# The mLSTM's queries and keys in 12 blocks of 128 features shared by heads, the decays' products one to a step

## The chip, the cores and the metric

The kernel runs on one core of one Trainium2 chip. The metric is the device time of a whole execution in microseconds: 1609.09 us, the median of three runs (1609.03 to 1609.48). What follows is about a stretch of some 125 us in the middle of it.

## What is computed

Two transformer blocks run over one sequence of 256 positions with 1024 features. The first has two layers; its second layer mixes positions with an mLSTM of 4 heads of 192 features, and this is the part that changes. Cut to that part:

```
u = x @ w_in_mlstm                      # 256 x 3336: q 768, k 768, v 768, o 768, gates 8, memory query 256
qk = silu(causal_dwconv(qk, qk_conv_w)) # 4 taps over positions, one weight per feature and tap
q, k = split(qk)                        # 4 heads of 192 features each
log_d = bcum[t] - bcum[s] + log_i[s]    # decay of position s seen from t, causal, stabilised
sc = (q_h . k_h * 192**-0.5) * exp(log_d - m)
h  = (sc @ v_h) / max(|sum(sc)|, exp(-m))
h  = layer_norm(h, per head) * head_norm_g
tok = sigmoid(o_pre) * h
x  = layer_norm(alpha * x + [tok, memory attention] @ w_out)
```

Silu and the taps work feature by feature, so it does not matter to them which features share a tile. Only `q_h . k_h` needs the 192 features of one head.

## The kernel before

Every weight matrix is cut by hand into a list of tiles (`weight_tiles`), of at most 128 x 2048 values, and the four engines walk this one list. SP fetches a tile into one of 4 `raw` buffers. ScalarE (ACT) rounds it to `whi`, VectorE (DVE) forms the rest `wlo`, and each has 3 buffers, so a tile can be prepared when TensorE (PE) is done with the tile three before it. Preparation runs two tiles ahead (`LOOK`). Each product is then made of three matmuls (high x high, high x low, low x high). Each engine's program is written out in order, and waits are on counters (`need.wait_ge`); what stands behind a waiting instruction on the same engine waits too.

PE's results go to 8 PSUM banks. The first four (`psw`) are handed out in turn by `bank(...)`: who claims one waits until the result that was in it four claims before has been taken out. The last four (`psy`) hold the wide results (`big_rows`).

Around the change the order is this. Gates and memory query; four tiles of values (`big_rows("v")`); the queries and keys; four tiles of output gates (`big_rows("o")`); then four tiles of the output projection (`big_rows("out1")`), the second of which waits for the finished heads. For queries and keys, head h and part 0 (q) or 1 (k) is one weight tile of 192 columns, so 8 tiles. `pair` on PE (L782 to L788) makes from it two blocks of 96 features x 256 positions in one bank: 2 blocks x 8 row blocks x 3 products = 48 matmuls of 256 columns. `head` on ACT (L1293) copies both blocks to `zp` and writes the last tap into `qk`; `head` on DVE (L1891) adds the other three taps with six instructions; `head_silu` (L1307) applies Silu in place. `qk[h % 2]` has two buffers. Between two tiles each engine does one entry of its list `steps`:

- `turn`, `value`, `finish`: the memory attention of the same layer, one head to a step.
- `weights(h)`: PE spreads the decay row of head h over the partitions (L751), ACT makes Exp of it twice (L1285), into `wt`; POOL then clears what is not causal (L2392). Before, all four heads are in the first step.
- `attend(h)`: PE multiplies keys and queries of head h (L757), DVE scales the product with `wt` into `sc` (L1904).
- `states(h)`: PE multiplies `sc` and values (L768), DVE forms the denominators and the statistics, ACT the divided copy `hb` between them (L1912, L1312), POOL normalises `hb` by the statistics, head after head and behind all four `weights` (the loop at L2403).

After the last `states`, ACT makes the sigmoid of the output gates (L1338), DVE multiplies it with the normalised heads in four pieces (L1942, L1944), PE turns the product (`mlstm_turned`, `headT`), ACT and DVE split it into high and low (`mhi`, `mlo`), and the second tile of `out1` can start. ACT functions come from tables: where Exp and Silu follow each other, an ACT_TABLE_LOAD stands between; copies need none.

Of the kernel before, what the change touches and what calls it, by code (L numbers as in the profile page):

```python
# [11 lines left out]
T = 256  # L12
# [15 lines left out]
def weight_tiles():  # L28
    tiles = []
# [93 lines left out]
PARAMS = [("conv_w", 18), ("qkconv", 64), ("conv_dw", 124), ("conv_b", 4), ("conv_g", 4), ("conv_lb", 4),  # L123
# [132 lines left out]
def program(nc, A, out):  # L256
# [5 lines left out]
    with ctx:  # L262
# [124 lines left out]
        zp = [arena.take(2 * 259).rearrange("p (b n) -> p b n", b=2)[0:96] for _ in range(2)]  # L387
        qk = [[arena.take(2 * T).rearrange("p (b n) -> p b n", b=2)[0:96] for _ in range(2)], [hf[0:96, s, :, :] for s in range(2)]]
# [110 lines left out]
        def tensor(e):  # L499
# [235 lines left out]
            def mlstm_mixer():  # L735
# [21 lines left out]
                def attend(h):  # L757
                    q_, k_ = qk[h % 2]
                    b = bank("attend", h)
                    for part in range(2):  # L760
                        need.wait_ge(*act.at("qk", h, part))
                    for f in range(2):
                        mm(b[:, 0:256], k_[:, f, 0:128], q_[:, f, :], f == 0, f == 1)
                    for f in range(2):
                        ins = mm(b[:, 256:384], k_[:, f, 128:256], q_[:, f, 128:256], f == 0, f == 1)
                    ins.then_inc(*pe.up(("bank", ("attend", h))))

                def states(h):  # L768
# [371 lines left out]
        def scalar(e):  # L1140
# [132 lines left out]
            def mlstm_mixer():  # L1273
# [19 lines left out]
                def head(h, part):  # L1293
                    b = place["head", h, part]
                    q_ = qk[h % 2][part]
                    need.wait_ge(*pe.at("bank", ("head", h, part)))
                    if h:
                        need.wait_ge(*dve.at("taps", h - 1, part))
                    copy(zp[part][:, :, 3:259], blocks(b[0:96, :], 256)).then_inc(*act.up(("zp", h, part)))
                    if h > 1:  # L1300
                        need.wait_ge(*pe.at("bank", ("attend", h - 2)))
                    for f in range(2):
                        blk = 8 * part + 2 * h + f
                        ins = copy(q_[:, f, :], b[0:96, 256 * f:256 * f + 256], scale=qwt[0:96, blk, 3:4])
                        ins.then_inc(*act.up(("tap3", h, part, f), *([took(("head", h, part))] if f else [])))

                def head_silu(h, part):  # L1307
                    q_ = qk[h % 2][part]
                    need.wait_ge(*dve.at("taps", h, part))
                    e.activation(q_, q_, ACT.Silu).then_inc(*act.up(("qk", h, part)))  # L1310
# [14 lines left out]
                steps = [lambda: (turn(1, 0), [weights(h) for h in range(4)]), lambda: turn(1, 1), lambda: turn(1, 2),  # L1325
# [1346 lines left out]
```

## Time and profile before

| | |
|---|---|
| median of three runs | 1609.09 us |
| the profiled execution, its own time | 1608.99 us |
| its span in the profile | 1607.2 us |
| PE, DVE, ACT, POOL busy, share of the span | 96%, 71%, 56%, 6% |
| mean granted clock of TensorE | 0.986 |
| the mLSTM's queries and keys | 721.5 to 784.2 us of the span |

The span is what the profile covers; the 1.8 us between it and the execution's own time lie around it. Times in the rows below are from the span's start. In a timeline a row merges instructions of one kind that follow each other: start, duration, engine, line, operation, what is written and read, how many, and in brackets how long the engine stood idle before it and on whom. Matmuls are pipelined: one of 256 columns is shown as 0.28 us long, but the next starts 0.12 us after it, so the spacing of starts is what a matmul costs.

### The profile page before, as it was taken

The page shows a single profiled execution, that of the slowest core. Times are in us where ns is not written, and L with a number is a line of the kernel's source. Part 1 is how long each engine was busy: PE and PEld are TensorE (multiplying, and loading weights), DVE is VectorE, ACT ScalarE, POOL GpSimd, SP SyncE. Part 2 cuts the span into 40 slices and gives each one's busy share as a digit, 9 for nine tenths or more (in the row PEclk, how much of TensorE's full clock was granted, in tenths as well). Part 3 has the DMA queues.
Part 4 walks back from the last instruction along what each step waited for, and adds up shares of the span by engine and source line. Part 5 has one row for each costly group of instructions (what it writes and reads, how often), then busy time and mean ns, then how long its engine had stood idle before and what let it go on. Part 6 is the DMA issues. An engine that isn't in the chain of part 4 may idle for free.

```text
span 1607.2 us, 22098 instructions
## 1 busy us (share of the span) xinstructions
PE 1543.8 (96%) x8926; PEld 1358.6 (85%) x8926; DVE 1138.4 (71%) x1628; ACT 897.7 (56%) x1356; POOL 101.8 (6%) x137
## 2 busy tenths in 40 slices
PE   7999999999999999999999999798999989999996
PEld 6888899888888888889978888797999778888885
DVE  5666666666667666655776566769867878989997
ACT  5455454455545555456545555444456657777774
POOL 0000000000000000001300000042002320000000
PEclk9999999999999999999999999899999999999998
DMA  9655454555555555343455554335334659999992
GB/s 359 211 191 197 159 196 162 195 218 197 186 183 198 196 183 191 138 148 101 160 207 222 189 197 162 133 125 210 131 106 164 234 210 350 354 347 345 359 368 103
DMA packets 48059, 332.99 MB, mean 207 GB/s; under 512 B 5712, under 2 KB 5840, under 8 KB 10192
## 3 DMA queue, kind: packets, MB, share of 16 engines
q1 hardware_dynamic: 46496, 321.43, 55.0%
q0 software_dynamic: 1456, 10.09, 1.6%
q8 instruction: 72, 1.18, 0.3%
q14 instruction: 35, 0.29, 0.1%
HBM read 330.45 MB, written 1.05 MB: 206 GB/s over the span
## 4 chain that ended last, share of the span: by engine, by line
PE 83%; DVE 10%; ACT 3%; POOL 1%; issue 1%; DMA 0%; SPq 0%; DVEq 0%; ACTq 0%; POOLq 0%
PE psw L505 54%; PE psy L505 28%; DVE wlo L1650 4%; DVE kT L2037 2%; PE psw L508 1%; ACT whi L1147 1%; POOL ar L2434 1%; DVE xs L1659 0%; DMA raw<-in_ws 0%; ACT xs L1147 0%; ACT ar L1147 0%; DVE x L1733 0%; POOL rstd L2354 0%; DVE gsel L2227 0%; DVE x L1746 0%
## 5 line engine op out<-in xcount | busy, mean ns | idle before, releaser
L1650 DVE TENSOR_TENSOR wlo<-raw,whi 128x1024 fp32r<-128x1024 f32 (+2 forms) x552 | 640.5, 1206 | 192.2 <-ACT whi L1147 186.7
L505 PE MATMUL psw<-xs,whi 128*128 128x512 f32 (+3 forms) x2544 | 687.3, 345 | 18.5 <-DVE wlo L1650 8.5
L1147 ACT ACTIVATE whi<-raw 128x1024 fp32r<-128x1024 f32 (+2 forms) x552 | 540.0, 1031 | 150.2 <-PE psy L505 107.0
L505 PE MATMUL psw<-xs,wlo 128*128 128x256 f32 (+2 forms) x1928 | 516.3, 282 | 2.1 <-DVE xs L1659 2.1
L505 PEld LDWEIGHTS psw<-xs,whi 128*128 128x128 f32 (+2 forms) x2544 | 427.4, 187 | 68.8 <-DVE wlo L1650 8.5
L505 PEld LDWEIGHTS psw<-xs,wlo 128*128 128x128 f32 (+2 forms) x1928 | 362.9, 188 | 17.4 <-issue 2.6
L505 PE MATMUL psw<-whi,xs 128*128 128x512 f32 (+1 forms) x704 | 178.9, 365 | 6.3 <-DVE xs L1659 5.1
L505 PE MATMUL psy<-whi,hhi 128*128 128x512 f32 x472 | 158.0, 390 | 0.0
L505 PE MATMUL psy<-whi,hlo 128*128 128x512 f32 x472 | 157.8, 389 | 0.0
L505 PE MATMUL psy<-wlo,hhi 128*128 128x512 f32 x472 | 157.7, 389 | 0.0
L505 PEld LDWEIGHTS psw<-whi,xs 128*128 128x128 f32 x704 | 126.0, 190 | 27.6 <-issue 2.6
L1147 ACT ACTIVATE ar<-psw 128x256 f32<-128x256 f32 (+3 forms) x127 | 56.3, 445 | 144.7 <-PE psw L505 131.4
L505 PE MATMUL psw<-wlo,xs 128*128 128x512 f32 (+1 forms) x352 | 106.6, 362 | 0.0
L505 PEld LDWEIGHTS psy<-whi,hlo 128*128 128x128 f32 x472 | 88.6, 188 | 18.5
L505 PEld LDWEIGHTS psy<-wlo,hhi 128*128 128x128 f32 x472 | 88.6, 188 | 18.4
L505 PEld LDWEIGHTS psy<-whi,hhi 128*128 128x128 f32 x472 | 88.6, 188 | 17.4
L1147 ACT ACTIVATE hf<-psw 128x256 f32<-128x256 f32 x82 | 31.0, 384 | 116.7 <-PE psw L505 116.7
L1688 DVE TENSOR_TENSOR hf<-hf,psw 128x256 f32<-128x256 f32 x82 | 34.0, 418 | 77.6 <-ACT hf L1147 77.6
L2354 POOL TENSOR_TENSOR rstd<-ve,mhalf 128x1 f32<-128x1 f32 x18 | 12.6, 699 | 1163.6 <-DVE ve L1739 1163.6
L1650 DVE TENSOR_TENSOR wlo<-ar,whi 128x1024 fp32r<-128x1024 f32 x64 | 74.4, 1222 | 4.9 <-ACT whi L1147 4.9
L505 PEld LDWEIGHTS psw<-wlo,xs 128*128 128x128 f32 x352 | 66.7, 190 | 10.4
L1693 DVE TENSOR_TENSOR ar<-ar,psw 128x256 f32<-128x256 f32 x82 | 34.3, 418 | 54.5 <-ACT ar L1147 54.5
(303 smaller groups left out, 1624.2 us busy)
## 6 DMA issues: line engine op xcount, KB each, us to landing
raw<-in_ws SPq DMA_DIRECT2D x252, 1024.0 KB, 4.8
ar<-in_ws SPq DMA_DIRECT2D x32, 1024.0 KB, 6.5
raw<-in_ws SPq DMA_DIRECT2D x17, 768.0 KB, 4.3
gb<-in_ln POOLq DMA_DIRECT2D x8, 1024.0 KB, 6.1
raw<-in_ws SPq DMA_DIRECT2D x4, 672.0 KB, 3.9
ar<-in_memT SPq DMA_DIRECT2D x2, 1024.0 KB, 13.7
ar<-in_xT SPq DMA_DIRECT2D x2, 512.0 KB, 5.4
raw<-in_ws SPq DMA_DIRECT2D x2, 512.0 KB, 6.3
```

The source lines that it names most:

```text
L505: return e.matmul(o, l, rr, start=start, stop=stop)
L508: return e.transpose(o, i, ident[0:n, 0:n])
L1147: return e.activation(o, i, ACT.Copy, **k)
L1650: e.tensor_tensor(wlo[i % NS][:, c0:c1], raw_t[slot[i]][:, c0:c1], whi[i % NS][:, c0:c1].bitcast(f32), ALU.subtract).then_inc(*made.up((i, ...
L1688: e.tensor_tensor(hf[:, s, j, :], hf[:, s, j, :], place["fgate", f, c, j][:, 0:256], ALU.add).then_inc(*dve.up(("fgate", f, c, j), took((" ...
L1693: then(e.tensor_tensor(corr[j], corr[j], place["up", f, c, j][:, 0:256], ALU.add), took(("up", f, c, j)))
L2037: ins = e.scalar_tensor_tensor(out=ca[:, b, :], in0=zc[:, b, tap:tap + 256], scalar=dwt[:, b, tap:tap + 1], in1=ca[:, b, :], op0=ALU.mult, ...
L2354: e.tensor_tensor(rstd[:, t:t + 1], ve[:, t:t + 1], mhalf[:, 0:1], ALU.pow).then_inc(*pool.up(("rstd", n, t)))
L2434: then(e.tensor_tensor(dst[:, lo:272], src[:, lo:272], src[:, lo - step:272 - step], ALU.add))
```

## The change

Queries and keys are made in tiles of 256 columns, j = 0 to 2, each for q and k: 6 tiles of two blocks of 128 features. A head's 192 features are then one whole block and half of another: head 0 has block 0 and the first half of block 1, head 1 the second half of block 1 and block 2, and so on. `attend(h)` still makes two products per result, over 128 and over 64 features instead of twice 96. The tap weights are laid out by 128 (`qkconv` shrinks from 64 to 48 columns). There are six steps instead of eight: `weights(h)` goes one head to a step (steps 0, 1, 3, 4), `attend(2)`, `attend(3)` stand together behind the first tile of output gates and `states(2)`, `states(3)` together behind the second. As `qk` has two buffers, tile pair 2 overwrites pair 0, and ACT's write of its last tap waits for `attend(1)`.

```diff
-    for h in range(4):
+    for j in range(3):
         for part in range(2):
-            n = 768 * part + 192 * h
-            tiles.append(("w_in_mlstm", (0,), 0, 8, n, n + 192))
+            n = 768 * part + 256 * j
+            tiles.append(("w_in_mlstm", (0,), 0, 8, n, n + 256))
...
                 def attend(h):
-                    q_, k_ = qk[h % 2]
+                    rows = [(192 * h, 192 * h + 128), (192 * h + 128, 192 * h + 192)] if h % 2 == 0 else [
+                        (192 * h, 192 * h + 64), (192 * h + 64, 192 * h + 192)]
                     b = bank("attend", h)
                     for part in range(2):
-                        need.wait_ge(*act.at("qk", h, part))
-                    for f in range(2):
-                        mm(b[:, 0:256], k_[:, f, 0:128], q_[:, f, :], f == 0, f == 1)
...
+                        need.wait_ge(*act.at("qk", (192 * h + 191) // 256, part))
+                    at = [(qk[r0 // 256 % 2], r0 // 128 % 2, r0 % 128, (r1 - 1) % 128 + 1) for r0, r1 in rows]
+                    for f, ((q_, k_), blk, p0, p1) in enumerate(at):
+                        mm(b[:, 0:256], k_[p0:p1, blk, 0:128], q_[p0:p1, blk, :], f == 0, f == 1)
...
-                steps = [lambda: (turn(1, 0), [weights(h) for h in range(4)]), lambda: (value(1, 0), turn(1, 1)),
-                         lambda: (attend(0), value(1, 1), turn(1, 2)), lambda: (states(0), value(1, 2), turn(1, 3)),
-                         lambda: (attend(1), value(1, 3)), lambda: (states(1), finish(1)), lambda: attend(2), lambda: states(2)]
-                for h in range(4):
+                steps = [lambda: (turn(1, 0), weights(0)), lambda: (value(1, 0), turn(1, 1), weights(1)),
+                         lambda: (attend(0), value(1, 1), turn(1, 2)), lambda: (states(0), value(1, 2), turn(1, 3), weights(2)),
+                         lambda: (attend(1), value(1, 3), weights(3)), lambda: (states(1), finish(1))]
+                for j in range(3):
                     for part in range(2):
-                        pair(("head", h, part), Tile("w_in_mlstm", 768 * part + 192 * h), xhi, xlo, x_rows(4), m=96)
+                        pair(("head", j, part), Tile("w_in_mlstm", 768 * part + 256 * j), xhi, xlo, x_rows(4))
                         steps.pop(0)()
                 big_rows("o", "w_in_mlstm", 4, xhi, xlo, lambda j, k: x_rows(4)(k), splits, 2304,
-                         {0: lambda: attend(3), 1: lambda: states(3)})
+                         {0: lambda: (attend(2), attend(3)), 1: lambda: (states(2), states(3))})
...
-                    copy(zp[part][:, :, 3:259], blocks(b[0:96, :], 256)).then_inc(*act.up(("zp", h, part)))
-                    if h > 1:
-                        need.wait_ge(*pe.at("bank", ("attend", h - 2)))
...
+                    copy(zp[part][:, :, 3:259], blocks(b[:, :], 256)).then_inc(*act.up(("zp", j, part)))
+                    if j > 1:
+                        need.wait_ge(*pe.at("bank", ("attend", 1)))
...
-                steps = [lambda: (turn(1, 0), [weights(h) for h in range(4)]), lambda: turn(1, 1), lambda: turn(1, 2),
-                         lambda: (states(0), turn(1, 3)), lambda: None, lambda: (states(1), finish(1)), lambda: None, lambda: states(2)]
...
+                steps = [lambda: (turn(1, 0), weights(0)), lambda: (turn(1, 1), weights(1)), lambda: turn(1, 2),
+                         lambda: (states(0), turn(1, 3), weights(2)), lambda: weights(3), lambda: (states(1), finish(1))]
...
-                w.rows(4, {0: lambda: attend(3), 1: lambda: states(3)})
+                w.rows(4, {0: lambda: (attend(2), attend(3)), 1: lambda: (states(2), states(3))})
```

(The first two lists of steps are PE's and ACT's; DVE's loses its last two entries, `attend(2)` and `states(2)`, in the same way.)

On ACT, the first two tiles of queries and keys. L1289 and L1290 are the Exps of one head's decays, L1310 the Silu. Before:

```order
L1147 ACTIVATE ar<-psw 96x2x256 [waits s_pe]
L1147 ACTIVATE ar<-psw,par 96x256 x2
L1147 ACTIVATE ar<-psw 128x512 [waits s_pe]
L1289 ACTIVATE ar<-psw,ar 128x256 [waits s_pe]
L1290 ACTIVATE ar<-psw,ar 128x128
...
L1289 ACTIVATE ar<-psw,ar 128x256 [waits s_pe]
L1290 ACTIVATE ar<-psw,ar 128x128
L1310 ACT_TABLE_LOAD
L1310 ACTIVATE ar<-ar 96x512 [waits s_dve]
```

Now (the same lines are L1291, L1292 and L1313, and the copies are L1149):

```order
L1149 ACTIVATE ar<-psw 128x2x256 [waits s_pe]
L1149 ACTIVATE ar<-psw,par 128x256 x2
L1149 ACTIVATE ar<-psw 128x512 [waits s_pe]
L1291 ACTIVATE ar<-psw,ar 128x256 [waits s_pe]
L1292 ACTIVATE ar<-psw,ar 128x128
L1313 ACT_TABLE_LOAD
L1313 ACTIVATE ar<-ar 128x512 [waits s_dve]
...
L1149 ACTIVATE ar<-psw,par 128x256 x2
L1149 ACTIVATE ar<-psw 128x512 [waits s_pe]
L1291 ACT_TABLE_LOAD
L1291 ACTIVATE ar<-psw,ar 128x256 [waits s_pe]
L1292 ACTIVATE ar<-psw,ar 128x128
L1313 ACT_TABLE_LOAD
L1313 ACTIVATE ar<-ar 128x512 [waits s_dve]
```

The three later heads' Exps have moved behind later tiles, and each is now enclosed by two table loads; six loads are added in all.

On PE, the work between the first two tiles; the product that spreads a head's decay row is `psw<-ar 128x256`. Before:

```order
L508 MATMUL psw<-par,gb 128x128 [waits s_dve]
L508 MATMUL psw<-par,gb 128x128 x3
L505 MATMUL psw<-ar 128x256 [waits s_pool,s_act]
L505 MATMUL psw<-ar 128x256 [waits s_act] x3
L505 MATMUL psw<-xs,whi 96x256 [waits s_wlo,s_act]
```

Now:

```order
L508 MATMUL psw<-par,gb 128x128 [waits s_dve]
L508 MATMUL psw<-par,gb 128x128 x3
L505 MATMUL psw<-ar 128x256 [waits s_pool,s_act]
L505 MATMUL psw<-xs,whi 128x256 [waits s_wlo,s_act]
...
L505 MATMUL psy<-vm,ar 128x64 [waits s_act]
L505 MATMUL psy<-vm,ar 128x64 x3
L508 MATMUL psw<-par,gb 128x128 x4
L505 MATMUL psw<-ar 128x256
L505 MATMUL psw<-xs,whi 128x256 [waits s_wlo,s_act]
```

The products of all four heads stood here, three of them behind waits for ACT; now one stands here, without the waits, and the other three have gone behind later tiles.

## Rows read from the trace of the kernel before

**Rows 1.** Busy time by engine, part 1 of the page.

```profile
PE 1543.8 (96%) x8926; PEld 1358.6 (85%) x8926; DVE 1138.4 (71%) x1628; ACT 897.7 (56%) x1356; POOL 101.8 (6%) x137
```

**Rows 2.** Timeline of PE, 128-feature tile of the memory query, and what follows.

```profile
695.09 0.40 PE L505 MATMUL psw<-xs,whi 128*128 128x256 f32 x2
...
700.85 0.52 PE L505 MATMUL psy<-whi,xs 128*128 128x384 f32 x2
```

**Rows 3.** Timeline of PE, queries and keys, first steps.

```profile
721.54 0.48 PE L505 MATMUL psw<-xs,whi 128*96 128x256 f32 x2
...
727.83 1.12 PE L505 MATMUL psw<-ar 4*128 4x256 f32 x4
...
729.95 1.36 PE L505 MATMUL psw<-ar 4*128 4x256 f32 x4 [1.00 <-ACT ar L1147]
...
731.25 0.74 PE L505 MATMUL psw<-xs,whi 128*96 128x256 f32 x2
...
738.32 1.00 PE L505 MATMUL psy<-vm,ar 128*128 128x64 f32 x8
...
739.53 0.48 PE L505 MATMUL psw<-xs,whi 128*96 128x256 f32 x2
...
745.26 1.47 PE L505 MATMUL psw<-ar 96*128 96x256 f32 x8
```

**Rows 4.** Stretches: from:to, length, busy of PE, PEld, DVE, ACT, POOL, PEclk, DMA.

```profile
731.00:732.00 1.00, 1.00 (x4) 0.76 (x4) 1.00 (x4) 1.00 (x4) 0.93 (x3) 0.50 0.52 197
...
804.00:808.00 4.00, 2.92 (x13) 2.44 (x14) 3.86 (x9) 2.72 (x4) 0.73 (x2) 1.00 1.01 360
```

**Rows 5.** Timeline of ACT, queries and keys.

```profile
728.57 0.61 ACT L1147 ACTIVATE ar<-psw 96x512 f32<-96x512 f32 x1
...
729.76 0.62 ACT L1147 ACTIVATE ar<-psw 128x512 f32<-128x512 f32 x1
...
732.05 0.54 ACT L1289 ACTIVATE ar<-psw,ar 128x256 f32<-128x256 f32 x1
...
732.86 1.28 ACT L1310 ACT_TABLE_LOAD   x1
...
734.16 0.63 ACT L1310 ACTIVATE ar<-ar 96x512 f32<-96x512 f32 x1
...
742.08 0.63 ACT L1310 ACTIVATE ar<-ar 96x512 f32<-96x512 f32 x1 [1.67 <-DVE ar L1900]
...
757.66 0.73 ACT L1147 ACTIVATE r<-psw,ar 128x192 f32<-128x192 f32 x2 [2.63 <-DVE ar L1917]
...
796.83 2.00 ACT L1147 ACTIVATE whi<-raw 128x1024 fp32r<-128x1024 f32 x2
```

**Rows 6.** Timeline of DVE, taps of one tile.

```profile
754.70 2.46 DVE L1900 SCALAR_TENSOR_TENSOR hf<-ar,par,hf 96x256 f32<-96x256 f32 x6 [2.53 <-ACT hf L1147]
```

**Rows 7.** Timeline of POOL, heads 2 and 3.

```profile
789.98 4.33 POOL L2405 TENSOR_SCALAR r<-r,ar 128x192 f32<-128x192 f32 x2
...
797.90 0.71 POOL L2403 TENSOR_TENSOR ar<-ar,mhalf 128x2 f32<-128x2 f32 x1 [3.60 <-DVE ar L1925]
...
798.72 5.39 POOL L2405 TENSOR_SCALAR r<-r,ar 128x192 f32<-128x192 f32 x2
```

**Rows 8.** Timeline of DVE, after the last head.

```profile
807.49 0.56 DVE L1944 TENSOR_TENSOR r<-r,ar 128x384 f32<-128x384 f32 x1
...
807.97 2.35 DVE L1650 TENSOR_TENSOR wlo<-raw,whi 128x1024 fp32r<-128x1024 f32 x2
...
811.91 1.89 DVE L1659 TENSOR_TENSOR mlo<-psw,mhi 128x512 fp32r<-128x512 f32 x3 [1.59 <-ACT mhi L1147]
```

**Rows 9.** Timeline of PE, states of head 3 and output projection.

```profile
794.44 1.14 PE L505 MATMUL psw<-ar 128*128 128x193 f32 x6
...
795.28 0.65 PE L505 MATMUL psy<-whi,xs 128*128 128x384 f32 x2
...
812.75 0.70 PE L505 MATMUL psy<-whi,mhi 128*128 128x512 f32 x2 [0.63 <-DVE mlo L1659]
```

More of the change, by code:

```diff
@@ L386, in program @@
         qwt = P("qkconv").rearrange("p (b w) -> p b w", w=4)
-        zp = [arena.take(2 * 259).rearrange("p (b n) -> p b n", b=2)[0:96] for _ in range(2)]
-        qk = [[arena.take(2 * T).rearrange("p (b n) -> p b n", b=2)[0:96] for _ in range(2)], [hf[0:96, s, :, :] for s in range(2)]]
+        zp = [arena.take(2 * 259).rearrange("p (b n) -> p b n", b=2) for _ in range(2)]
+        qk = [[arena.take(2 * T).rearrange("p (b n) -> p b n", b=2) for _ in range(2)], [hf[:, s, :, :] for s in range(2)]]
         sc = [arena.take(384) for _ in range(2)]
@@ L1291, in weights, with head, head_silu @@
                                  scale=-1.0).then_inc(*act.up(("decay", h), took(("decay", h))))
[L1293 to L1298, printed above, removed]
-                    copy(zp[part][:, :, 3:259], blocks(b[0:96, :], 256)).then_inc(*act.up(("zp", h, part)))
-                    if h > 1:
-                        need.wait_ge(*pe.at("bank", ("attend", h - 2)))
-                    for f in range(2):
[L1303 to L1310, printed above, removed]
+                def head(j, part):
+                    b = place["head", j, part]
+                    q_ = qk[j % 2][part]
+                    need.wait_ge(*pe.at("bank", ("head", j, part)))
+                    if j:
+                        need.wait_ge(*dve.at("taps", j - 1, part))
+                    copy(zp[part][:, :, 3:259], blocks(b[:, :], 256)).then_inc(*act.up(("zp", j, part)))
+                    if j > 1:
+                        need.wait_ge(*pe.at("bank", ("attend", 1)))
+                    for f in range(2):
+                        blk = 6 * part + 2 * j + f
+                        ins = copy(q_[:, f, :], b[:, 256 * f:256 * f + 256], scale=qwt[:, blk, 3:4])
+                        ins.then_inc(*act.up(("tap3", j, part, f), *([took(("head", j, part))] if f else [])))
+                def head_silu(j, part):
+                    q_ = qk[j % 2][part]
+                    need.wait_ge(*dve.at("taps", j, part))
+                    e.activation(q_, q_, ACT.Silu).then_inc(*act.up(("qk", j, part)))
                 def states(h):
@@ L1324, in mlstm_mixer @@
                              blocks(place["y", "v", 2 * t + i][:, 0:384], 192)).then_inc(*act.up(took(("y", "v", 2 * t + i)), ("va",)))
-                steps = [lambda: (turn(1, 0), [weights(h) for h in range(4)]), lambda: turn(1, 1), lambda: turn(1, 2),
-                         lambda: (states(0), turn(1, 3)), lambda: None, lambda: (states(1), finish(1)), lambda: None, lambda: states(2)]
-                for h in range(4):
+                steps = [lambda: (turn(1, 0), weights(0)), lambda: (turn(1, 1), weights(1)), lambda: turn(1, 2),
+                         lambda: (states(0), turn(1, 3), weights(2)), lambda: weights(3), lambda: (states(1), finish(1))]
+                for j in range(3):
                     for part in range(2):
                         w.tile()
-                        head(h, part)
+                        head(j, part)
                         steps.pop(0)()
-                        head_silu(h, part)
-                w.rows(4, {1: lambda: states(3)})
+                        head_silu(j, part)
+                w.rows(4, {1: lambda: (states(2), states(3))})
                 for t in range(2):
@@ L1889, in decay_columns, with head @@
                     e.tensor_copy(ac, blocks(place["decays",][:, 0:16], 8)).then_inc(*dve.up(took(("decays",))))
-                def head(h, part):
-                    q_ = qk[h % 2][part]
+                def head(j, part):
+                    q_ = qk[j % 2][part]
                     need.wait_ge(*pool.at("zp", part))
@@ L1895, in head @@
                         for f in range(2):
[L1896 to L1897 removed]
+                            blk = 6 * part + 2 * j + f
+                            need.wait_ge(*act.at("tap3", j, part, f))
                             if s:
[L1899 to L1900 removed]
+                                need.wait_ge(*dve.at("tap", j, part, s - 1, f))
+                            e.scalar_tensor_tensor(out=q_[:, f, :], in0=zp[part][:, f, s:s + 256], scalar=qwt[:, blk, s:s + 1],
                                                    in1=q_[:, f, :], op0=ALU.mult,
[L1902 removed]
+                                                   op1=ALU.add).then_inc(*dve.up(("tap", j, part, s, f), ("taps", j, part)))
                 def attend(h):
@@ L1929, in mlstm_mixer @@
                 steps = [lambda: None, lambda: None, lambda: attend(0), lambda: states(0), lambda: (attend(1), scale(1)),
-                         lambda: (states(1), finish(1)), lambda: attend(2), lambda: states(2)]
-                for h in range(4):
+                         lambda: (states(1), finish(1))]
+                for j in range(3):
                     for part in range(2):
                         w.tile()
-                        head(h, part)
+                        head(j, part)
                         steps.pop(0)()
-                w.rows(4, {0: lambda: attend(3), 1: lambda: states(3)})
+                w.rows(4, {0: lambda: (attend(2), attend(3)), 1: lambda: (states(2), states(3))})
                 need.wait_ge(*hn_in.at("hn"))
```

13 lines of the change are left out of this document (4 added, 9 removed).

## The prediction

> **What bounds the kernel now.** I read the busy times first: TensorE (PE) works 96% of the span [rows 1], so time is won where PE has less to do or stops waiting. Then the PE timeline of the queries and keys, the only place the change touches. PE reaches them at 721.54. Up to the weights' products it runs without a gap; then come four such products (two at 727.83, two at 729.95, with 1.00 us of idle time between them that ended with ACT), and the second tile starts at 731.25 [rows 3]. Last, the other engines of the stretch: ACT works there in a long chain per tile (copy, last tap, copy of the memory probabilities, Silu) [rows 5], and DVE's three taps take 2.46 us [rows 6]. They follow PE, and PE asks for their results one step later. So the stage is PE's, but ACT is close behind.
>
> **Term 1, the matmuls: -11.3 us.** A 128-feature tile of 48 matmuls runs from 695.09 to 700.85, 5.76 us [rows 2]. A 96-feature one runs from 739.53 to 745.26, 5.73 us [rows 3]. Fewer output features make a matmul no cheaper, 0.12 us either way. Eight tiles at 5.73 are 45.8, six at 5.76 are 34.6. The difference is 11.3 us of PE, all on the path.
>
> **Term 2, the burst of decay products: -2.6 us.** Two heads' products, issued without waiting, take about 1.05 us, since four instructions of rows 3 run 0.26 us apart; so four heads would be done at 729.93, and the next tile starts at 731.25: 1.3 us of waits. That tile then takes 7.07 us, 731.25 to 738.32, instead of 5.73: 1.34 us more [rows 3]. The granted clock shows why: 0.50, the 1.2 GHz level, from 731 to 732 [rows 4]. Before it fell, PE had idled and worked on products with 4 rows. Now one product stands there, and its bank has been emptied before. Both parts go.
>
> **Term 3, ACT's longer chain: +2.4 us.** The decays' Exps now come one head to a step, each between a load of the Exp table and one of the Silu table: six loads more, at 1.28 us each [rows 5], 7.7 us of ACT. ACT and DVE also prepare tiles a third larger: two halves of 1024 take ACT 2.00 us [rows 5], so three quarters of it, 1.5, before. Three larger tiles are prepared before ACT gets to the first queries, 1.5 us of ACT together, and DVE's part of them also delays the score maxima for which ACT waits, by about as much as one tile's growth, 0.5. So I put ACT's first copy at 730.6 instead of 728.57 [rows 5]. From there the steps are laid end to end.
> - One head's Exps: 0.80 us, 732.05 to the load at 732.86 [rows 5]. First tile: copies 1.3, memory copy 0.6, Exps 0.8, load 1.3, Silu 0.6: done at 735.0. Second tile: preparation 1.95 (736.9), copies (738.2), memory copy (738.8), load, Exps and load 3.4 (742.2), Silu: 742.8.
> - PE: first tile to 727.3, transposes and one product 1.05, tile to 734.1, the value and transposes 1.2 (738.32 to 739.53) [rows 3] and a product 0.5, tile to 741.6. `attend(0)` needs the Silu of 742.8: PE waits 1.2 us. Before, that Silu began at 742.08 and PE came at 745.26 [rows 3, 5].
> - The same again at `attend(1)`. PE leaves the fourth tile at 751.2, does the states of head 0, value, transposes and a product (2.7), and the fifth tile ends at 759.7. ACT from 751.2: copies to 752.6, DVE's taps 2.46 [rows 6] to 755.0, denominators and divided copies 1.2 as from the end of the taps at 757.16 to 758.39 [rows 5, 6], memory copy, load, Exps, load, Silu: 760.9. PE waits 1.2 us.
>
> Bounds: nothing if ACT has caught up by then; at most 2.6 each, if both switches of a step fall wholly on PE. I take 1.2 twice, as the steps give it. Behind `attend(2)` there is none: one tile of output gates stands between it and the last queries, and the last step has no Exps.
>
> **Here the Trainium skill speaks against the change.** The row shows the load starting 0.01 us after the last Exp's end and Silu 0.02 us after the load's [rows 5]: 1.28 us in all. The page "ScalarE: Activation LUTs" (What ACT_TABLE_LOAD costs) gives about 1.28 us for the load and 1.38 for a drain, 2.66 for every switch, and advises doing all of one set before switching. By it ACT would get 16.0 us more instead of 7.7, and the sum would be about 1604.8.
>
> **Term 4, the end of the heads: +2.0 us.** Now `states(2)` and `states(3)` come together, so POOL gets its last two heads together. Output gate tile 3 starts at 795.28, 0.84 us after `states(3)` [rows 9], and POOL starts head 3 at 797.90 and is done at 804.11 [rows 7]. By terms 1 to 3 PE is about 11.5 us earlier at 795.28, at 783.8. Head 2's states are ready 0.84 us earlier than head 3's, and DVE needs about 2.2 for one head, so POOL starts head 2 at 785.3. It takes 0.8 and 4.33, until 790.5; head 3 another 0.8 and 5.39, until 796.7 [rows 7]. That is 7.4 us earlier than before, while PE is 11.5 earlier. DVE's last product ends at 808.05, then it prepares a tile (2.35), then writes the rest for which PE waits until 812.75 [rows 8, 9]. From 796.7 this gives 800.7, 803.0, and with the first rest 803.8 for PE, against 801.2 if nothing were late: 2.6. With POOL at 4.33 also for head 3 it is 1.5. I take 2.0; the bounds are 0.5 and 3.5, since POOL's pace changes with what DVE does.
>
> **At no cost.** The attend products over 128 and 64 instead of 96 and 96 rows: as many instructions, columns unchanged, under 1.5 us per head [rows 3]; a gain or loss of some 0.1. DMA: the same bytes in fewer transfers, issued four tiles ahead, six tiles of 5.8 us. ACT's last tap of pair 2 waits for `attend(1)`; PE is done with it while ACT still prepares a tile. Copies, taps and Silus, 8 sets before and 6 now, save work beside PE.
>
> **The sum.** -11.3 - 2.6 + 2.4 + 2.0 = -9.5 us. The profiled execution took 1608.99 for a span of 1607.2, 0.1 below the median; so 1599.5 for it and **1599.6** for the median. What follows in the kernel moves forward unchanged.
>
> **Rivals.**
> 1. *ACT has caught up* and term 3 is nothing: 1597.2. For it: idle time on ACT in these steps, 1.67 us before the Silu at 742.08 [rows 5]. Against: it is used in the sum already. Chance 0.08.
> 2. *The clock falls once or twice at the new waits.* A wait of 1.2 us, then attend products, narrow values and transposes, looks a little like what came before 731. Against it, 1.1 us of idle time in 804 to 808 left the clock at 1.00 [rows 4]. Price 1.3 us each as in term 2: 1600.9 or 1602.2. Chance 0.20.
> 3. *A switch of tables costs twice its row*, the page's rule: two switches stand before each of the two Silus for which PE waits, so 2 x 2.6 more: 1604.8. For it no row; the load of rows 5 shows 1.28. Chance 0.06, and with a fall of the clock on top it passes 1605.9.
> 4. *Slower: the low clock stays.* After the wait at `attend(0)`, with waits, small products and waits following, the clock stays at 1.2 GHz for the three remaining tiles and on. At half the clock a tile takes up to twice its 5.76 us. Break-even is at 1.7 tiles; with three, 17.2 us: 1616.8. Against: the fall at 731 was over within one tile, which cost only 1.34 [rows 3]. Chance 0.02.
>
> That the change doesn't do what it says (a 128-wide tile costs more, or the wider last block adds passes) is excluded by rows 2.
>
> **How the numbers follow.** Forecast 0.64, rivals 0.08, 0.20, 0.06, 0.02. The range runs from rival 1 to just over two falls of the clock, with term 4's bounds in it: 1597.0 to 1602.8; left out are rivals 3 and 4 and the coincidence of ends, some 0.15. A measurement of this kernel can tell about 0.2%, 3.2 us, from no change. Forecast, rivals 1 and 2 and a third of rival 3 are faster by more: 0.94. The rest of rival 3, with a fall of the clock: 0.04 within. Slower 0.02.
>
> **What would show it.** PE busy down by about 11 us; no idle time and clock 1.00 between the first two tiles; waits of about 1.2 us on ACT's Silu (L1313) ahead of `attend(0)` and `attend(1)`; six more loads of 1.28 us; the second output projection tile waiting 3 to 5 us behind the turned heads, for a chain that begins with POOL's head 3. No wait at the attends, one over 2.5 us, or a PEclk of 0.50 past 740 would make term 3 wrong; POOL done with head 3 more than 8.5 us earlier than before would make term 4 wrong.

## The result, and the profile after

| | before | the change |
|---|---|---|
| median | 1609.28 us (4 runs, 1609.03 to 1610.63) | 1599.66 us (4 runs, 1598.42 to 1601.15) |
| ratio | | 0.9936 (95% interval 0.9924 to 0.9949) |
| the profiled execution: its own time, span | 1608.99, 1607.2 us | 1601.15, 1599.3 us |
| mean granted clock | 0.986 | 0.989 |

The forecast was 1599.6, so the sum was met. Its terms were not: both savings and both costs in it were put too large, a cost that had been put at nothing was 2.45 us, and these misses nearly cancelled. That the two numbers agree to 0.1 us is luck. The page first, the row of busy times:

```profile
PE 1535.0 (96%) x8830; PEld 1345.6 (84%) x8830; DVE 1132.9 (71%) x1612; ACT 902.3 (56%) x1350; POOL 97.3 (6%) x137
```

PE is busy 8.8 us less than in [rows 1]; about 11 had been forecast. Single executions of one kernel lie up to 4.3 us apart (the nine of the kernel before on one chip from 1607.01 to 1611.32), and the profiled one of the change is the slowest of its four. A stage can be compared more sharply than a whole execution, so all that follows is read from one stretch. It begins with the last score products of the memory attention (`psw<-kT`, 720.49 before, 720.34 now), which stand just ahead of the first tile of queries and keys, and ends with the first matmul of the second output projection tile (812.75 in [rows 9], 804.05 now). It took 92.26 us and takes 83.71, 8.55 less. From there to the end of the span it is 194.5 us before (1607.2 - 812.75) and 195.3 now (1599.3 - 804.05), a difference of the size that one kernel shows from run to run.

PE in that stretch, in the timeline:

```profile
721.39 0.51 PE L505 MATMUL psw<-xs,whi 128*128 128x256 f32 x2
...
727.25 0.60 PE L508 MATMUL psw<-par,gb 128*128 128x128 f32 x4
727.78 0.69 PE L505 MATMUL psw<-ar 4*128 4x256 f32 x2
728.41 0.50 PE L505 MATMUL psw<-xs,whi 128*128 128x256 f32 x2
...
734.27 1.00 PE L505 MATMUL psy<-vm,ar 128*128 128x64 f32 x8
...
736.26 0.50 PE L505 MATMUL psw<-xs,whi 128*128 128x256 f32 x2
...
742.77 2.13 PE L505 MATMUL psw<-ar 128*128 128x256 f32 x8 [0.50 <-ACT ar L1313]
744.83 1.10 PE L505 MATMUL psy<-vm,ar 128*128 128x64 f32 x8
...
761.47 0.67 PE L505 MATMUL psw<-ar 64*128 64x256 f32 x2 [0.53 <-ACT hf L1313]
...
763.44 1.00 PE L505 MATMUL psy<-vm,ar 128*128 128x64 f32 x8
...
776.90 0.67 PE L505 MATMUL psw<-hf 128*128 128x256 f32 x2 [0.30 <-ACT ar L1313]
...
786.56 0.66 PE L505 MATMUL psy<-whi,xs 128*128 128x384 f32 x2
...
804.05 0.70 PE L505 MATMUL psy<-whi,mhi 128*128 128x512 f32 x2 [0.63 <-DVE mlo L1662]
```

Start to start, a tile is 5.86 us (721.39 to 727.25, and again 728.41 to 734.27). Between the first two tiles stand only the transposes and one product of 4 rows (727.78, 0.63 us), and nothing is waited for there; in [rows 3] this place had four products and 1.00 us of idle time. At 742.77 and 761.47 the brackets show the new waits for Silu. `attend(0)` takes from 742.77 to 744.83, 2.06 us, where it took 1.31 (745.26 in [rows 3] to 746.57). One line of the kernel before shows that end, the other two the transposes ahead of the burst and ahead of the third tile:

```profile
727.29 0.60 PE L508 MATMUL psw<-par,gb 128*128 128x128 f32 x4
...
739.16 0.61 PE L508 MATMUL psw<-par,gb 128*128 128x128 f32 x4
...
746.57 1.00 PE L505 MATMUL psy<-vm,ar 128*128 128x64 f32 x8
```

The clock was full where it had been 0.50 in [rows 4], and full around the new waits. Stretches of the change, with the columns of [rows 4]:

```profile
728.00:732.00 4.00, 4.00 (x32) 3.67 (x32) 2.42 (x3) 4.00 (x8) 0.00 (x0) 1.00 0.35 141
732.00:736.00 4.00, 4.00 (x35) 3.76 (x33) 2.38 (x6) 3.69 (x7) 0.82 (x2) 1.00 0.55 197
...
740.00:744.00 4.00, 3.50 (x24) 2.66 (x23) 1.16 (x4) 3.97 (x6) 0.54 (x2) 1.00 0.46 181
...
760.00:764.00 4.00, 3.47 (x22) 2.52 (x22) 1.83 (x2) 3.63 (x6) 0.00 (x0) 1.00 0.01 4
```

ACT, from its copy of the first tile on, and at the second one, where the Exps of head 1 stand between two table loads:

```profile
730.35 0.63 ACT L1149 ACTIVATE ar<-psw 128x512 f32<-128x512 f32 x1
...
738.66 1.28 ACT L1291 ACT_TABLE_LOAD   x1
739.95 0.47 ACT L1291 ACTIVATE ar<-psw,ar 128x256 f32<-128x256 f32 x1
740.32 0.36 ACT L1292 ACTIVATE ar<-psw,ar 128x128 f32<-128x128 f32 x1
740.70 1.28 ACT L1313 ACT_TABLE_LOAD   x1
742.00 0.63 ACT L1313 ACTIVATE ar<-ar 128x512 f32<-128x512 f32 x1
```

The end of the heads, POOL and then DVE:

```profile
788.20 0.71 POOL L2406 TENSOR_TENSOR ar<-ar,mhalf 128x2 f32<-128x2 f32 x1 [7.06 <-DVE ar L1918]
789.01 2.01 POOL L2408 TENSOR_SCALAR r<-r,ar 128x192 f32<-128x192 f32 x2
...
792.26 4.45 POOL L2408 TENSOR_SCALAR r<-r,ar 128x192 f32<-128x192 f32 x2
```

```profile
800.47 2.35 DVE L1653 TENSOR_TENSOR wlo<-raw,whi 128x1024 fp32r<-128x1024 f32 x2
```

POOL is done with head 3 at 796.71 (792.26 + 4.45).

### The profile page after: what moved, and what is told of

It reads as the page before. It is cut to its first block, busy times and chain, and to the rows that moved or that the text cites. A ratio compares the mean times of both kernels' runs of the same rounds, so it can differ in the third digit from the quotient of the medians.

```text
span 1599.3 us, 21882 instructions
## 1 busy us (share of the span) xinstructions
PE 1535.0 (96%) x8830; PEld 1345.6 (84%) x8830; DVE 1132.9 (71%) x1612; ACT 902.3 (56%) x1350; POOL 97.3 (6%) x137
## 3 DMA queue, kind: packets, MB, share of 16 engines
HBM read 330.44 MB, written 1.05 MB: 207 GB/s over the span
## 4 chain that ended last, share of the span: by engine, by line
PE 81%; DVE 11%; ACT 4%; POOL 1%; issue 1%; DMA 0%; SPq 0%; DVEq 0%; ACTq 0%; POOLq 0%
PE psw L505 53%; PE psy L505 27%; DVE wlo L1653 4%; DVE kT L2040 2%; PE psw L508 1%; ACT whi L1149 1%; POOL ar L2437 1%; DVE xs L1662 1%; DMA raw<-in_ws 0%; ACT ar L1149 0%; ACT xs L1149 0%; DVE ar L1903 0%; DVE x L1736 0%; POOL rstd L2357 0%; DVE gsel L2230 0%
## 5 line engine op out<-in xcount | busy, mean ns | idle before, releaser
L1653 DVE TENSOR_TENSOR wlo<-raw,whi 128x1024 fp32r<-128x1024 f32 (+3 forms) x548 | 640.0, 1213 | 195.8 <-ACT whi L1149 190.3
L505 PE MATMUL psw<-xs,whi 128*128 128x512 f32 (+2 forms) x2480 | 674.2, 346 | 18.6 <-DVE wlo L1653 8.6
L1149 ACT ACTIVATE whi<-raw 128x1024 fp32r<-128x1024 f32 (+3 forms) x548 | 539.8, 1037 | 148.7 <-PE psy L505 106.7
L505 PE MATMUL psw<-xs,wlo 128*128 128x256 f32 (+1 forms) x1896 | 506.5, 281 | 2.1 <-DVE xs L1662 2.1
L505 PEld LDWEIGHTS psw<-xs,whi 128*128 128x128 f32 (+1 forms) x2480 | 419.6, 189 | 69.7 <-DVE wlo L1653 8.6
L505 PEld LDWEIGHTS psw<-xs,wlo 128*128 128x128 f32 (+1 forms) x1896 | 359.3, 189 | 17.4 <-issue 2.6
L1149 ACT ACTIVATE ar<-psw 128x256 f32<-128x256 f32 (+3 forms) x125 | 55.3, 444 | 136.6 <-PE psw L505 124.0
L1149 ACT ACTIVATE hf<-psw 128x256 f32<-128x256 f32 x82 | 31.2, 386 | 116.4 <-PE psw L505 116.3
```

The source lines that it names most:

```text
L505: return e.matmul(o, l, rr, start=start, stop=stop)
L1149: return e.activation(o, i, ACT.Copy, **k)
L1653: e.tensor_tensor(wlo[i % NS][:, c0:c1], raw_t[slot[i]][:, c0:c1], whi[i % NS][:, c0:c1].bitcast(f32), ALU.subtract).then_inc(*made.up((i, ...
```

## Experiments

Each stretch below is measured as above, in one profiled execution. Times are medians in us, ratios are against runs of the kernel before on the same chip; the kernels ran on several chips. The rows of a product are what it sums over, the first number in `128x256`.

| kernel | stretch | time (runs) | ratio, 95% interval |
|---|---|---|---|
| before | 92.26 | 1609.28 (4) | |
| the change | 83.71 | 1599.66 (4) | 0.9936, 0.9924 to 0.9949 |
| blocks of 128 alone | 86.77 | 1602.49 (4) | 0.9954, 0.9937 to 0.9971 |
| decays one to a step alone | 91.31 | 1607.91 (10) | 0.9989, 0.9979 to 0.9998 |
| no table switches | 82.37 | 1598.40 (2) | 0.9928, 0.9908 to 0.9948 |
| whole blocks in attend | 81.37 | 1596.99 (2) | 0.9919, 0.9899 to 0.9939 |
| 96 and 64 rows in the old layout | 96.87 | 1613.21 (1) | |
| 64 rows only in the old layout | 93.62 | 1609.74 (1) | |
| equal row counts side by side | 82.95 | 1598.51 (5) | 0.9932, 0.9918 to 0.9945 |
| decays early, attend a step later | 82.25 | 1597.95 (5) | 0.9926, 0.9912 to 0.9939 |
| the same, decays in two pairs | 81.14 | 1597.32 (1) | |
| the same, ACT's last step turned round | 79.93 | 1594.95 (5) | 0.9915, 0.9901 to 0.9928 |

The first theory was that the attend products cost more because consecutive products differ in rows, that a table load costs the 1.28 us that its row shows and no more, and that the burst is worth more with the larger blocks than without. The rivals: the 2.45 us come from something else at these places (the clock, a late buffer), and the two halves of the change add up.

### The two halves of the change

Blocks of 128, all decays again in the first step (PE's and ACT's lists):

```diff
-                steps = [lambda: (turn(1, 0), weights(0)), lambda: (value(1, 0), turn(1, 1), weights(1)),
+                steps = [lambda: (turn(1, 0), [weights(h) for h in range(4)]), lambda: (value(1, 0), turn(1, 1)),
```

> The stretch is the time on TensorE from the last score product of the memory attention to the first matmul of the second output projection tile: 92.3 us before, 83.7 with the change. This kernel has the blocks of 128 but all four heads' decay products and Exps in the first step again. Theory: the burst stalls TensorE until ACT has emptied the banks, now later than before, since ACT starts its first copy at 730.4 instead of 728.6, so the second tile starts at about 733 instead of 728.4, at the low clock for some 3 us; against that three products of 0.63 us are no longer between later tiles and the waits for Silu at attend(0) and attend(1), 0.66 and 0.68 us, are gone: stretch 86.5, between 85.5 and 87.5, 2 to 3 us slower than the change. Rival: spreading the decays is worth nothing, because the six table loads it adds cost as much as the burst: within 0.5 us of the change's 83.7.

Blocks of 96 as before, the decays at steps 0, 1, 3 and 4:

```diff
-                steps = [lambda: (turn(1, 0), [weights(h) for h in range(4)]), lambda: (value(1, 0), turn(1, 1)),
+                steps = [lambda: (turn(1, 0), weights(0)), lambda: (value(1, 0), turn(1, 1), weights(1)),
```

> The kernel before, with eight tiles of 96 as it had, and only the decays one head to a step. Theory: the burst and its low clock go (3.42 us between the transposes and the second tile become 0.63, the tile takes 5.73 instead of 7.07), three products of 0.63 us come in later steps, and ACT, which has smaller tiles to prepare and starts 1.8 us earlier than with the change, keeps ahead of TensorE: no wait at the attends, stretch 92.3 - 2.8 - 1.3 + 1.9 + 0.3 = 90.4. Rival: the six table loads alone make the waits at attend(0) and attend(1), whatever the tiles' size: then 91.5 or more.

Measured: 86.77 us (86.5 expected) and 91.31 us (90.4 expected). So the blocks alone give 5.49, the decays alone 0.95, and both together 8.55, 2.1 more than the two added. PE with the blocks alone:

```profile
727.71 1.13 PE L505 MATMUL psw<-ar 4*128 4x256 f32 x4
731.67 2.07 PE L505 MATMUL psw<-ar 4*128 4x256 f32 x4 [2.83 <-ACT ar L1149]
```

Its clock there, in the same columns as above:

```profile
728.00:732.00 4.00, 1.17 (x5) 0.71 (x5) 2.51 (x3) 4.00 (x9) 0.00 (x0) 0.77 0.31 129
732.00:736.00 4.00, 4.00 (x15) 3.16 (x15) 2.31 (x6) 3.97 (x11) 2.65 (x8) 0.50 0.58 197
```

With blocks of 128, ACT is later with its first copies, and the burst waits 2.83 us for it instead of 1.00; then PE runs at 0.50 through the rest of the burst, two products in 2.0 us, and on through the first third of the matmuls of the next tile, which takes 7.31 us (not shown: 733.67 to 740.98) instead of 5.86. With blocks of 96, PE meets ACT a second time, at `attend(1)`:

```profile
741.52 1.47 PE L505 MATMUL psw<-ar 96*128 96x256 f32 x8
...
759.27 1.55 PE L505 MATMUL psw<-hf 96*128 96x256 f32 x8 [0.62 <-ACT hf L1310]
```

There is no wait at `attend(0)`, and the tile before `attend(1)` had its last matmul at 758.37: some 0.8 us are lost on Silu. That is why the decays alone came out 0.9 above what I expected. The rival of that run was half right: the loads make the wait at `attend(1)` with tiles of 96 too, the one at `attend(0)` only with the larger tiles.

### ACT's table loads

The Exps of heads 1 to 3 become copies, so that no function of the Exp table stands there:

```diff
+                    if h:
+                        copy(wt[:, h, 0:256], b[:, 0:256], scale=ac[:, 0, h:h + 1])
+                        copy(wt[:, h, 256:384], b[:, 128:256], scale=ac[:, 1, h:h + 1])
...
+                        return
```

> The change, with the Exps of the decays of heads 1 to 3 replaced by copies scaled by the same column, so that none of the six added table loads is left; the decays of those heads are no decays any more. Theory: ACT is done 2.6 us earlier in each step with decays, the waits at attend(0) and attend(1) vanish (0.66 and 0.68 us), and the stretch is 83.7 - 1.3 = 82.4. Rival: the waits come from the larger tiles (ACT's and DVE's preparation) and stay: 83.7.

```profile
742.35 2.05 PE L505 MATMUL psw<-ar 128*128 128x256 f32 x8
...
760.37 0.70 PE L505 MATMUL psw<-ar 64*128 64x256 f32 x2
```

Both waits are gone and the stretch is 1.34 us shorter. The change's own two waits add up to the same: tile starts at 736.26 and (not shown) 754.94, plus 5.86 each, would have let the attends start at 742.12 and 760.80; they started at 742.77 and 761.47, 0.65 and 0.67 later. So all of what six more loads cost PE is these 1.3 us, of 7.7 that they take on ACT. The third wait for Silu, 0.30 us at `attend(2)` (776.90), is no part of it: it is 0.29 us without the loads, and the kernel before has one of 0.22 at `attend(3)` (not shown: 788.86). The gate tile and the wait behind it take 4.7 us in all three.

### The rows of consecutive products

`attend` with 128 rows in all of its products, in both blocks that hold a part of the head. A head's product then takes in features of its neighbour, so this kernel serves for its time alone:

```diff
-                    at = [(qk[r0 // 256 % 2], r0 // 128 % 2, r0 % 128, (r1 - 1) % 128 + 1) for r0, r1 in rows]
+                    at = [(qk[r0 // 256 % 2], r0 // 128 % 2, 0, 128) for r0, r1 in rows]
```

> The change, with the attend products over all 128 rows of both blocks of a head instead of 128 and 64, so that a head's product takes in 64 features of its neighbour. More rows, same number of instructions and columns. Theory A (what costs is a change in the number of rows between products that follow each other, about 0.2 us each, four to a head): the four attends take 5.1 us together as before, not 7.6, and the stretch is 83.7 - 2.5 = 81.2. Theory B (the blocks of 128 are dearer than those of 96, or products out of two tile pairs are): no change, 83.7, or more.

```profile
742.73 1.55 PE L505 MATMUL psw<-ar 128*128 128x256 f32 x8 [0.49 <-ACT ar L1313]
744.11 1.00 PE L505 MATMUL psy<-vm,ar 128*128 128x64 f32 x8
```

`attend(0)` takes 1.38 us instead of 2.06, at the same place, behind the same wait, with as many products and columns. The stretch is 2.34 shorter. The weight loads show where the time is. The change, then the kernel before:

```profile
742.74 0.30 PEld L505 LDWEIGHTS psw<-ar 128*128 128x128 f32 x2 [0.67 <-ACT ar L1313]
743.37 0.29 PEld L505 LDWEIGHTS psw<-ar 64*128 64x128 f32 x2 [0.33 <-issue]
744.00 0.71 PEld L505 LDWEIGHTS psw<-ar 128*128 128x128 f32 x4 [0.33 <-issue]
```

```profile
745.15 1.40 PEld L505 LDWEIGHTS psw<-ar 96*128 96x128 f32 x8
```

With 96 rows in each, the eight loads run on without a gap. In the change there is an idle time of 0.33 us, ended by no other engine, before the load of 64 rows and again before the one of 128; with whole blocks the eight loads take 1.38 us without one (not shown).

Then the same question with neither the blocks nor the moved decays: in the kernel before, the second block of each head with 64 rows instead of 96, and, in a second kernel, both with 64.

```diff
-                    for f in range(2):
-                        mm(b[:, 0:256], k_[:, f, 0:128], q_[:, f, :], f == 0, f == 1)
+                    for f, p in ((0, 96), (1, 64)):
+                        mm(b[:, 0:256], k_[0:p, f, 0:128], q_[0:p, f, :], f == 0, f == 1)
```

> The kernel before, where each attend product takes the second block of 96 features over its first 64 rows only (a third of it is left out): sequence 96, 64, 96, 64 rows. Less work than before. Theory A (changes in the number of rows cost about 0.2 us each): every attend takes 2.0 us instead of 1.3, stretch 92.3 + 2.6 = 94.9. Rival (rows don't matter, or fewer are cheaper): 92.3 or less.

> The kernel before, with both blocks of every attend product over their first 64 rows: sequence 64, 64, 64, 64. It tells a change in the number of rows from a short product: theory A gives a cost only on entering and leaving, 0.2 to 0.4 us per head, so stretch 92.6 to 93.9 and attends of 1.3 us; if 64 rows are dear by themselves, it is at least that of the kernel with 96 and 64.

```profile
745.17 2.06 PE L505 MATMUL psw<-ar 96*128 96x256 f32 x8
747.16 1.11 PE L505 MATMUL psy<-vm,ar 128*128 128x64 f32 x8
```

```profile
745.79 1.57 PE L505 MATMUL psw<-ar 64*128 64x256 f32 x8
747.29 1.10 PE L505 MATMUL psy<-vm,ar 128*128 128x64 f32 x8
```

With fewer rows in half of the products `attend(0)` takes 1.99 us, with fewer in all of them 1.50, and with 96 it took 1.31. So it is not the work, nor small products as such, but each change between many rows and 64. Counted from an attend's first product to what follows it, there are four such changes in 96/64/96/64 and then 128 (0.68 us more), one in 64/64/64/64 and then 128 (0.19), four in the change's 128/64/128/64 and then 128 (0.68 more than whole blocks): 0.17 to 0.19 us each. Between 96 and 128 rows nothing shows. What stands beside an attend pays a little too: the eight value products behind `attend(0)` take 0.94 us where it ends with 64 rows, and 0.84 where it ends with 96 or 128. The stretch of the second kernel, 93.62, is within the 92.6 to 93.9 that were expected, but its attends are 1.5 us long, not 1.3. The stretch of the first, 96.87, is 4.6 above before, not 2.6: the four attends take 2.9 us more, two groups of value products 0.2, and the other 1.5 is the clock. The second half of the burst and the tile behind it take 1.54 us longer than in the kernel before, and the mean clock from 728 to 736 was 0.57, where the kernel before has 0.79. This place stands ahead of the first product that the edit touches, so how long the clock stays low there differs by that much without a reason in the edit, and a stretch with such a fall in it, read from one execution, is uncertain by as much; the 92.26 of the kernel before has one in it too.

Next, an order that has fewer such changes and computes the same:

```diff
+                    at = at if h % 2 == 0 else at[::-1]
...
-                    for f, ((q_, k_), blk, p0, p1) in enumerate(at):
+                    for f, ((q_, k_), blk, p0, p1) in enumerate(at[::-1]):
```

> The change, with the same attend products in another order: 128, 64, 64, 128 rows instead of 128, 64, 128, 64 (or 64, 128, 64, 128), for all four heads. The numbers are the same. Theory A: two changes of rows per head instead of four, so 0.35 us less each: attends 6.3 us together, stretch 83.7 - 1.3 = 82.4. Theory B (the products themselves are dearer): 83.7.

```profile
742.84 1.94 PE L505 MATMUL psw<-ar 128*128 128x256 f32 x8 [0.49 <-ACT ar L1314]
744.61 1.00 PE L505 MATMUL psy<-vm,ar 128*128 128x64 f32 x8
```

128/64/64/128, two changes: 1.77 us, 0.39 above whole blocks, 0.20 each. The stretch is 0.76 shorter than the change's, where 1.3 was expected. The expectation counted eight changes fewer; it is six, since in the change `attend(2)` and `attend(3)` stand side by side and already meet with 64 rows each. By the stretch the six are 0.13 us each, somewhat less than at `attend(0)`. Against the kernel before it is 0.9932; by whole executions it can't be told from the change, whose interval overlaps.

### A better place for the decays

Both waits stand on the switches of tables. All six added loads go if the Exps of the decays are made in the last value step, before any Silu. Two heads share a bank, and `attend(0)` is done one step later:

```diff
-                         {... 3: lambda: score(1, 3)})
-                steps = [lambda: (turn(1, 0), weights(0)), ...
+                         {... 3: lambda: (score(1, 3), weights(0), weights(2))})
+                steps = [lambda: turn(1, 0), lambda: (value(1, 0), turn(1, 1)),
+                         lambda: (value(1, 1), turn(1, 2)), lambda: (attend(0), value(1, 2), turn(1, 3)),
+                         lambda: (states(0), attend(1), value(1, 3)), lambda: (states(1), finish(1))]
```

> The change, with that order of rows, the decays of two heads in one bank, all four products and Exps directly behind the last score product and so ahead of the first Silu (no added table load), and attend(0) one step later. Theory: attends 1.3 us less, no waits for Silu at attend(0) and attend(1) (1.3), products in one run of 2.2 us and three transposes that are no longer followed by a 4-row product (0.7 together): stretch 83.7 - 3.3 = 80.4, the fastest kernel. Rival: the last heads' chain through POOL and DVE to the second output projection tile, which has 0.4 us to spare by the profile, gives part of it back: 81 to 82.

It gave 82.25, 1.8 more than expected. PE:

```profile
719.89 1.99 PE L505 MATMUL psw<-ar 4*128 4x256 f32 x8
721.81 0.79 PE L505 MATMUL psw<-xs,whi 128*128 128x256 f32 x2
...
774.12 0.67 PE L505 MATMUL psw<-hf 128*128 128x256 f32 x2 [0.94 <-ACT ar L1318]
```

Its clock from 721 to 726:

```profile
721.00:722.00 1.00, 1.00 (x6) 0.61 (x5) 0.67 (x1) 1.00 (x2) 0.00 (x0) 0.93 1.04 442
722.00:723.00 1.00, 1.00 (x5) 1.00 (x6) 1.00 (x2) 0.25 (x1) 0.00 (x0) 0.50 0.53 221
725.00:726.00 1.00, 1.00 (x9) 1.00 (x9) 0.00 (x0) 1.00 (x6) 0.00 (x0) 0.87 0.65 229
```

The first tile took 7.36 us (721.81 to 729.17) instead of 5.86: the clock fell again, this time with PE busy all the time before. Ahead of the fall stand four score products of 64 rows (718.83) and four decay products of 4 rows, 3 us in all. The mean clock was 0.986 in all five executions of this kernel and 0.987 or 0.988 in those of the two other kernels of the table that ran five times, so the fall is not one execution's alone, though that difference is small. And `attend(2)` waits 0.94 us, instead of 0.30, for a Silu that ACT's divided copies had pushed back: with the Exps out of the way there is still this wait. The first was tested by splitting the decays:

```diff
-                          3: lambda: (score(1, 3), weights(0), weights(2))})
-                steps = [lambda: turn(1, 0), lambda: (value(1, 0), turn(1, 1)),
+                          3: lambda: (score(1, 3), weights(0))})
+                steps = [lambda: (turn(1, 0), weights(2)), lambda: (value(1, 0), turn(1, 1)),
```

> The kernel with decays of two heads in one bank and attend(0) one step later, in which TensorE did not idle and yet fell to the low clock (0.50 from 722 to 725) behind the last score product and four decay products in a row, 3 us of products of 64 and 4 rows. Here the second two decay products stand behind the first tile of queries, as does their Exp, still ahead of the first Silu. If products of few rows in a row bring the clock down, the first tile takes 5.8 us again instead of 7.4 and the stretch from the last score product to the second output projection tile is 82.3 - 1.5 + 0.2 = 81.0. If the fall had another cause (chance of the moment), it stays at 82.3.

81.14, 1.1 less (81.0 expected), and the first tile takes 5.86 us again (not shown: 722.22 to 728.08). This is one execution. Then also the second, ACT making its last Silu before the divided copies of that step:

```diff
-                        steps.pop(0)()
+                        step = steps.pop(0)
+                        if steps:
+                            step()
                         head_silu(j, part)
+                        if not steps:
+                            step()
```

> The same, and in the last step of queries and keys ACT applies the Silu before it does the denominators' copies and the memory's, instead of after. TensorE waited 0.94 us for this Silu at attend(2). Theory: that wait goes, stretch 81.0 - 0.9 = 80.1, the fastest of all, about 1597. Rival: the states of head 1, now later on ACT, hold up DVE's and POOL's chain to the second output projection tile, and 0.5 us or more comes back there.

```profile
719.91 1.12 PE L505 MATMUL psw<-ar 4*128 4x256 f32 x4
```

```profile
721.00:725.00 4.00, 4.00 (x34) 4.00 (x34) 3.13 (x4) 1.72 (x4) 0.00 (x0) 1.00 0.55 188
```

PE no longer waits at any attend. 79.93 us (80.1 expected), and 1594.95 for the whole kernel, the fastest of all: 4.7 below the change, of which the stretch shows 3.8. By the ratios against the kernel before, the two intervals still touch (0.9901 to 0.9928, and 0.9924 to 0.9949).

## Why the prediction was right, and where it was not

**Term 1, -11.3: -10.7.** Six tiles at 5.86 are 35.16; eight at 5.73 are 45.84. The 5.76 of [rows 2] held for a tile that follows other wide products. The tiles here follow transposes or other short products, and their first three matmuls take 0.1 us more than the next ones, in both kernels. So like for like it is 5.73 against 5.86, or 5.82 behind transposes alone (746.14 to 751.96): fewer features made a tile cheaper by some 0.1 us, which the prediction had put at 0.03.

**Term 2, -2.6: -2.2.** The clock's 1.34 are gone in full (1.00 in 728 to 736). Of the burst's 3.42 us (727.83 to 731.25 in [rows 3]) only 0.9 was saved: one product alone, which is two instructions, costs 0.63 us, not half of the 1.05 of two in a row, and there are four of them. At two places more than before the transposes ahead of such a product also cost 0.17 more; the sum below has that apart. What I didn't see is that the burst would have grown with the blocks: the kernel that leaves it where it was takes 3.06 us more (86.77 against 83.71).

**Term 3, +2.4: +1.3.** The mechanism and the places were right, each wait of 1.2 us was 0.66. ACT met its steps well, Silu ended at 742.63 (forecast 742.8), the one of `attend(1)` at 761.32 (760.9). It was PE that came later than forecast, by 0.5 and by 1.1 us, through the terms above and `attend(0)`. That there would be no wait behind was wrong: `attend(2)` waits 0.30 us, but so did `attend(3)` before, and the difference is nothing.

**Term 4, +2.0: nothing.** POOL was done with head 3 at 796.71, forecast 796.7, but by two errors: it began head 2 2.9 us later, with PE, and did its two pieces in 2.01 us instead of the 4.33 of [rows 7]. DVE's last product ended at 800.56, its tile at 802.82 and PE went on at 804.05, forecast 803.8. What failed is the other side of the comparison: PE's own way there. Gate tile 3 was put at 783.8 and stood at 786.56. The transposes then ran from 801.95, and PE waited 0.63 us behind them, as in [rows 9].

**"At no cost": +2.45.** This is the step that was wrong. The bound of 0.1 came from the number of instructions and columns, and from a row in which all products have 96 rows. In the trace of the change the four attends take 2.06, 1.97 and, the last two together, 3.56 us, 7.59 instead of 5.14. A sign of it was in the old trace, in rows that I had not compared: four transposes took 0.54 us where a product of 4 rows follows (727.29 to 727.83) and 0.37 where one of 128 does (739.16 to 739.53). The bound should have been taken from that, 0.2 for each place where the rows change: the attends have 14 such places in the change and none before, and with whole blocks, where all of them are gone, the stretch is 2.34 us shorter, 0.17 each.

The sum by what was measured: -10.7 - 2.2 + 1.3 + 0 + 2.45 + 0.3 (transposes) = -8.85, measured -8.55 in the stretch. The 0.3 between them is in the value products beside products of few rows (0.2 us more in four groups) and in the last two heads' states, 1.83 us together instead of 1.69. The median moved by 9.6; where the other 1.1 us are was not found, and the two profiled executions lie only 7.8 apart.

**The rivals.** *ACT has caught up*: no, two waits of 0.66 remain. *The clock falls at the new waits*: no. It stayed at 1.00 from 740 to 744 and from 760 to 764, with 0.50 and 0.53 us of idle time in them, and the tile behind `attend(0)` took 5.82 us. *A switch costs twice its row*: no. Exp began 0.01 us after the first load's 1.28, Silu 0.02 after the second's (738.66 to 742.00). The Trainium skill, page "ScalarE: Activation LUTs" (What ACT_TABLE_LOAD costs), adds a drain of 1.38 us to each switch; the trace shows none, and with all six loads removed the stretch fell by 1.34, not by the 6.5 that, by estimate, it would have been with rival 3's 5.2 on top. *The low clock stays*: no, it did not fall.

## What to carry to other kernels

When blocks are cut anew, count not only instructions and columns but also how often the number of rows changes between consecutive products; put equal ones side by side, or fill up to the whole block where the rest of it holds zeros (not tried here: the kernel with whole blocks took in the neighbour's features). A burst of narrow products that waits on another engine has a price that grows when that engine falls behind, so two edits that touch it must be costed together. Where two functions need different tables, make all calls of the one before the first of the other, and then look at what else stands ahead of the result: with the Exps ahead of all Silus PE no longer waited at `attend(0)` and `attend(1)`, but `attend(2)` still waited 0.94 us, until ACT made its last Silu ahead of its copies.

## What the runs showed that I had not expected

- A change between 64 rows and 96 or 128 in consecutive fp32 products costs 0.17 to 0.2 us, and the loads stand idle 0.33 us for it. Transposes ahead of a product of 4 rows cost 0.17 more than ahead of one of 128. Between 96 and 128 rows none was seen. The runs show the cost and where it stands, not what the engine does in that time.
- The clock fell to 0.50 with PE never idle, after 3 us of products of 64 and 4 rows; with half as many products of 4 rows there (719.91 in the last kernel) it stayed at 1.00. What exactly decides was not tried, and each is one profiled execution. In the kernel with the blocks alone it fell after 2.83 us of waiting among such products.
- POOL's two pieces of a head (128x192 each) took 2.01 us while DVE ran short instructions and 4.45 while it ran its large ones (790.32 on), 4.33 and 5.39 in [rows 7]. That DVE is the cause was not tested.
